# Turning the third of four squared MLP blocks with VectorE and ScalarE instead of TensorE, and taking the weight groups of the first down product in the order 0, 1, 3, 2

## The reference, cut to what matters

```python
u = _rmsnorm(h, norm_mlp_g)          # 256 x 2048
a = einsum('sd,df->sf', u, w_up)     # 256 x 8192
a = square(relu(a))
h = h + einsum('sf,fd->sd', a, w_down)
```

## Time and profile before

| | |
|---|---|
| median of 3 runs | 2249.17 us (2249.11 to 2249.85) |
| profiled execution, its own time | 2250.41 us |
| its span in the profile | 2248.7 us |
| granted TensorE clock, mean | 0.998 |
| instructions | 28778 |
| TensorE matmul busy | 2230.3 us |
| VectorE busy | 1642.7 us |
| ScalarE busy | 1149.5 us |

### The profile page before, as it was taken

The page is one execution under the profiler, slowest core; times in us unless marked ns, Lnnn a source line. Parts: engine busy times, 40 slices in busy tenths (PEclk is TensorE's granted clock), DMA queues, the critical chain, the costliest instruction groups (busy, mean ns, idle before and its releaser), DMA issues.

```text
span 2248.7 us, 28778 instructions
## 1 busy us (share of the span) xinstructions
PE 2230.3 (99%) x10115; PEld 1841.4 (82%) x10115; DVE 1642.7 (73%) x2156; ACT 1149.5 (51%) x1500; POOL 226.6 (10%) x369
## 2 busy tenths in 40 slices
PE   9999999999999999999999999999999999999998
PEld 7888888888888888888878877878888888888886
DVE  7998789988988988998788774656555545555556
ACT  5446457446546645645565744544443344434444
POOL 0111001111111111111011000001110011100110
PEclk9999999999999999999999999999999999999999
DMA  8983678988887898887678663656665666655663
GB/s 310 325 270 123 207 249 297 326 275 296 293 303 271 277 314 279 276 275 259 219 238 256 224 198 113 226 168 203 209 198 191 220 197 203 206 189 189 207 192 124
DMA packets 250109, 527.97 MB, mean 235 GB/s; under 512 B 22258, under 2 KB 22658, under 8 KB 248704
## 3 DMA queue, kind: packets, MB, share of 16 engines
q1 hardware_dynamic: 214256, 405.32, 54.7%
q0 software_dynamic: 33776, 116.17, 15.0%
q10 hardware_dynamic: 1952, 4.85, 0.6%
HBM read 517.87 MB, written 4.21 MB: 232 GB/s over the span
## 4 chain that ended last, share of the span: by engine, by line
PE 96%; DVE 2%; ACT 1%; issue 0%; DMA 0%; ACTq 0%; DVEq 0%; POOLq 0%
PE acc L1981 30%; PE acc L1985 30%; PE acc L1990 30%; PE tp L2053 1%; DVE wlo L1176 1%; PE acc L2004 0%; PE acc L2009 0%; PE acc L2014 0%; PE tp L2367 0%; PE tp L2385 0%; PE tp L2379 0%; PE acc L2037 0%; PE acc L2036 0%; PE acc L2035 0%; PE m L2174 0%
## 5 line engine op out<-in xcount | busy, mean ns | idle before, releaser
L609 ACT ACTIVATE whi<-wring 128x1024 fp32r<-128x1024 f32 x756 | 796.4, 1060 | 930.9 <-PE acc L1990 929.7
L1176 DVE TENSOR_TENSOR wlo<-wring,whi 128x1024 fp32r<-128x1024 f32 x754 | 909.6, 1225 | 439.5 <-ACT whi L609 438.2
L1981 PE MATMUL acc<-whi,xhi 128*128 128x512 f32 x2056 | 556.1, 392 | 0.1
L1985 PE MATMUL acc<-whi,xlo 128*128 128x512 f32 x2056 | 549.8, 389 | 0.0
L1990 PE MATMUL acc<-wlo,xhi 128*128 128x512 f32 x2056 | 549.7, 389 | 0.0
L1985 PEld LDWEIGHTS acc<-whi,xlo 128*128 128x128 f32 x2056 | 386.0, 188 | 80.7
L1990 PEld LDWEIGHTS acc<-wlo,xhi 128*128 128x128 f32 x2056 | 386.0, 188 | 80.4
L1981 PEld LDWEIGHTS acc<-whi,xhi 128*128 128x128 f32 x2056 | 383.2, 188 | 82.4 <-issue 4.7
L1218 DVE SCALAR_TENSOR_TENSOR macc<-mring,csil,macc 128x512 f32<-128x512 f32 x480 | 344.3, 749 | 36.0 <-DMA mring<-w_mod 30.1
L493 POOL DMA_DIRECT2D mring<-w_mod x192 | 139.2, 725 | 1101.2 <-DVE macc L1218 1054.2
L1981 PE MATMUL acc<-whi,ahi 128*128 128x512 f32 x608 | 163.5, 391 | 0.0
(11 more groups left out here) (296 smaller groups left out, 1335.2 us busy)
## 6 DMA issues: line engine op xcount, KB each, us to landing
wring<-w_up SPq DMA_DIRECT2D x216, 512.0 KB, 5.0
wring<-w_down SPq DMA_DIRECT2D x216, 512.0 KB, 5.7
mring<-w_mod POOLq DMA_DIRECT2D x192, 512.0 KB, 5.5
wring<-w_in SPq DMA_DIRECT2D x184, 512.0 KB, 5.0
wring<-w_gate SPq DMA_DIRECT2D x88, 512.0 KB, 4.4
wring<-w_out SPq DMA_DIRECT2D x64, 512.0 KB, 5.0
tmpT<-blk POOLq DMA_DIRECT2D x128, 32.0 KB, 3.2
gbig<-ctx_in POOLq DMA_DIRECT2D x2, 1024.0 KB, 6.5
```

The costliest lines, as they stand in the source:

```text
L609: act.activation(whi[:, piece_slot(c, piece), 0:half], wring[:, g4, piece * half:(piece + 1) * half], ACT.Copy).then_inc(hi_done, 1)
L1176: dve.tensor_tensor(wlo[:, h4, 0:half], wring[:, g4, piece * half:(piece + 1) * half], whi[:, h4, 0:half].bitcast(F32), ALU.subtract).then ...
L1981: pe.matmul(acc[:, 2 * pair + t, :], hi[:, tile, t * P:(t + 1) * P], whi[:, h4, w], start=(tile == starts), stop=False)
L1985: pe.matmul(acc[:, 2 * pair + t, :], lo[:, tile, t * P:(t + 1) * P], whi[:, h4, w], start=False, stop=False)
```

## The change

Block 2 is turned like blocks 0 and 1, by VectorE and ScalarE; only block 3 is left to TensorE. TensorE issues the 8 transposes of block 3 after group 16 instead of after group 17. The weights of the first down product (and of it alone) are loaded and multiplied in the order 0, 1, 3, 2, so that group 18 contracts over block 3 and group 19 over block 2. Ahead of the first group TensorE waits for the remainders of blocks 0 and 1, as before; ahead of group 18 it now waits for both `tp` banks, ahead of group 19 for the remainders of block 2. On ScalarE both late moves of block 2 stand between steps 16 and 17, and its rounding stands behind `round_banks` of block 3 after step 17. On VectorE, at step 17, `remain_banks` of block 3 stands first and `remain_relu` of block 2 behind it. The other edits are counts of the banks and of the blocks.

```diff
-MLP_MOVED = 2
+MLP_MOVED = 3
+MLP_ORDER = (0, 1, 3, 2)
...
-                    block_of(w_down, n * NB, kg0=i * 4)
+                    block_of(w_down, n * NB, kg0=i * 4, order=MLP_ORDER if n == 0 else None)
...
                     if 2 <= j <= MLP_MOVED + 1:
                         move_relu(2)
+                    if j == MLP_MOVED + 1:
+                        move_relu(3)
                     round_group(4 * j + 1)
                     if first and j == 0:
                         root(1)
+                    if 2 <= j <= MLP_MOVED:
+                        move_relu(3)
+                    if j == MLP_MOVED + 1:
+                        round_banks(xhi, 4 * MLP_MOVED, 2)
                     if 2 <= j <= MLP_MOVED + 1:
-                        move_relu(3)
                         round_relu(4 * (j - 2))
-                    if MLP_MOVED < j <= 4:
-                        round_banks(xhi, 4 * (j - 1), 2)
...
                     if g % 4 == 1 and 1 <= j <= 4:
+                        if j > MLP_MOVED:
+                            remain_banks(xhi, xlo, 4 * MLP_MOVED, 2)
                         if 2 <= j <= MLP_MOVED + 1:
                             remain_relu(4 * (j - 2))
                         if j <= MLP_MOVED:
                             turn_relu()
                         c.add("blk")
-                        if j > MLP_MOVED:
-                            remain_banks(xhi, xlo, 4 * (j - 1), 2)
...
                     for kg in range(3):
                         if j == 4 and kg == 0:
-                            pe.wait_ge(relu_lo, c.at("rs", KG * MLP_MOVED, KG))
-                        multiply(hi, lo, (kg,), 4, pair)
+                            pe.wait_ge(relu_lo, c.at("rs", KG * (MLP_MOVED - 1), KG))
+                        elif j == 4 and kg == 2:
+                            pe.wait_ge(tp_free, c.at("q", 2))
+                        order = MLP_ORDER if j == 4 else tuple(range(4))
+                        multiply(hi, lo, (order[kg],), 4, pair, order=order)
...
-                        if kg == 1 and MLP_MOVED < j <= 4:
-                            pe.wait_ge(blk_ready, c.at("blk", j))
+                        if kg == 0 and j == 4:
+                            pe.wait_ge(blk_ready, c.at("blk", 4))
                             turn_rows(blk, 2)
                         turn_ctx(4 * j + kg)
-                    if j == 4 or (first and j == 0):
+                    if first and j == 0:
                         pe.wait_ge(tp_free, c.at("q", 2))
-                    multiply(hi, lo, (3,), 4, pair)
+                    elif j == 4:
+                        pe.wait_ge(relu_lo, c.at("rs", KG * MLP_MOVED, KG))
+                    multiply(hi, lo, (order[3],), 4, pair, order=order)
```

## The result

The changed kernel takes 2275.03 us (median of 4 runs, 2274.89 to 2275.19), the kernel before in the same comparison 2249.51 us (2249.11 to 2251.09). The ratio is 1.0109, with a 95% interval of 1.0096 to 1.0121: 25.5 us slower. The forecast was 2267.8 us with a range of 2262 to 2272. The sign, the place and the length of the stop came as forecast; the time lies above the range.

The account below looks back on a forecast made before the run. The prediction took TensorE's matmuls to bound the kernel, busy 2230.3 of 2248.7 us. Stops of 18.9 less transposes of 3.6, plus 3.3 for the clock, gave +18.6 on 2249.17: 2267.8 us, range 2262 to 2272.

Parts of the forecast that it names:

- The transposes, 3.6 us won: On TensorE, block 2's 8 transposes go, 0.91 us in each of 4 chunks: 3.6 us less.
- The stop, 18.9 us: TensorE waits after group 17 for VectorE's backlogged `remain_banks`, 4.61 to 4.75 us a chunk: 18.9 us over four.
- that bare chain: Lower bound of the stop with VectorE free, 3.7 us; as the no-backlog rival 2260 us, chance 0.05.
- ScalarE ready by a hair: On ScalarE, block 3 is ready 5.38 us after its product, hidden by group 16's 5.44.
- No cost of `remain_relu`, no stop ahead of group 19: At VectorE's step 17, four `remain_relu`, 1.43 us together, lie beside group 18 and cost nothing.
- The clock, 3.3 us: TensorE's clock may fall at the four stops, 1.63 us each; half of 6.5 us taken, 3.3.
- TensorE busy for less: Expected sign in the changed profile: TensorE's busy time falls while the span grows; no size given.
- The sum: Stops of 18.9 less transposes of 3.6 give +15.3 us; with 3.3 for the clock, +18.6.
- the likeliest case: Stop ahead of group 18 bound by VectorE, no to four clock falls: 2264.5 to 2271.0 us, chance 0.84.
- the rival of the clock taking more: Clock falls at each stop and stays low twice as long, 3.3 us each: +28 us, 2277, chance 0.07.
- matmuls slow for more than 4 us after a stop: Sign on TensorE that would prove the clock term wrong: slow matmuls lasting over 4 us behind a stop.

Follow-up runs that it names:

- order alone: Kernel before with only the order 0, 1, 3, 2 and block 3's transposes after group 16; TensorE still turns block 2: 2275.76 us, ratio 1.0111.
- ScalarE first: Changed kernel with only ScalarE's rounding of block 3's banks moved ahead of its step 17: 2275.3 us, ratio 1.0111.
- VectorE first: Changed kernel with only VectorE's remainders of block 3's banks moved ahead of its step 17: 2266.21 us, ratio 1.0067.
- The run with 20 filling matmuls: Changed kernel with 20 small matmuls into an unused bank ahead of TensorE's wait at group 18: 2268.57 us, ratio 1.0079.
- the last version: Changed kernel with block 3's banks and block 2's strips taken ahead of step 17 on both engines: 2248.66 us, ratio 0.9993; timed again 2248.38 us, 0.9987.
- move alone: Changed kernel with the old group order 0, 1, 2, 3, and block 2 done ahead of block 3 at step 17: 2275.92 us, ratio 1.0112.
- the banks taken early: Changed kernel with only block 3's banks rounded and their remainders taken ahead of step 17, on both engines: 2250.73 us, ratio 1.0002.

## Why the prediction was wrong, point by point

- *The transposes, 3.6 us won*: right as a term, but only together with the stop. VectorE sets the time at which group 18 starts, so what TensorE saves ahead of it makes the stop longer by as much: order alone issues block 2's transposes, has a stop of 3.9 instead of 4.7 us, and starts group 18 at 417.70 against 417.56. With the stop removed, 2.0 and 2.6 us were measured.
- *The stop, 18.9 us*: 18.7 measured, at the place, by the releaser and for the reason given. ScalarE first and VectorE first confirm the two chains: 4.7 us by VectorE's queue, and behind it 3.1 to 3.2 us of lost time (3.0 of idle time) by ScalarE's. The prediction had 3.7 for that bare chain, with a remainder of weights in it that VectorE does not have to make first once its order is changed.
- *ScalarE ready by a hair*: right. The transposes start at 406.44, 0.04 after the set at 405.49 would have ended, and nothing follows from it.
- *No cost of `remain_relu`, no stop ahead of group 19*: right; TensorE's only waits in the chunks are the four.
- *The clock, 3.3 us*: **this is the step that failed**. I priced a fall at 1.63 us, from the one fall in the trace of before, and took half of four. I also described that place by two waits, 1.49 and 1.20 us; there is a third, of 1.08 us for VectorE's `h`, ahead of them (at 1511.11). The clock fell at all four stops, for 2.24, 1.71, 1.48 and 2.87 us, 8.3 in sum, and the fall at the opening of the second block's MLP cost 1.4 us more than before. That is 9.7 us for a term of 3.3. The one fall I had was near the cheap end of a spread of 1.5 to 3.0 us, and taking half had no row behind it. The run with 20 filling matmuls shows that the slow sets are the lowered clock: the same stop at a clock of 1.00 brings the next sets at their pace. For the same reason the sign "TensorE busy for less" did not come: it is busy for 6.8 us more. The Trainium skill ("TensorE: Matmul & The Clock Gate", HAM oscillation — how this bites in real kernels), which has a loop with such a wait pay for the return of the clock in every pass, was the better guide here: the loop paid in every pass, 1.5 to 2.9 us each time. With idle times of 3.0 and 2.3 us it paid in two passes of four.
- *The sum*: 15.3 was 15.1 by the trace. With 9.7 for the clock it would have been 2249.17 + 15.3 + 9.7 = 2274.2, against 2275.03. The measured case lies between the likeliest case and the rival of the clock taking more, for which I had taken double the price of one fall and a chance of 0.07. That rival's sign, matmuls slow for more than 4 us after a stop, was met at the first stop (4.96 us) and the fourth (6.50), and not at the other two.

What stays open is why the opening of the second block's MLP pays 1.4 us more in this kernel. Its code and its waits (1.49 and 1.20 us) are unchanged. In the run with ScalarE first the same place has two slow sets, of 1.87 and 1.47 us, in order alone it pays 3.0 us again, and in both profiled executions of the last version no set there is slow. So the price varies at a place that no edit touches, from nothing to 3.0 us, and the 1.4 may be the luck of two executions; no run isolates it. Nor does any run take out the doubled multiply-adds of steps 8 to 15: that VectorE's queue sets the end of the stop is shown, that these are what makes the queue late is read from the code and the timeline alone.

## What to carry to other kernels

When a consumer is moved forward by one step, the producers' place in their own queues must move too: here the transposes went one group earlier, but the two engines that pass their result on still took it behind a step that waits for the group just ended, or that comes late by their own load. Read for each new wait the time at which its last producer is done today, and subtract the time at which the consumer now wants it. And where this makes an engine of dense matmuls stop, price the clock with the stop, at every pass of the loop. Take for the price the whole spread of the falls that the traces show, and not a fraction of one.

## What the runs showed of the hardware that I had not expected

All counts here are of the stops in one profiled execution of each run. An idle time of TensorE ahead of dense matmuls made the granted clock fall to 0.50 in 12 of 12 cases at 4.5 to 4.8 us (the changed kernel, ScalarE first, move alone), in 4 of 4 at 3.7 us, in 2 of 4 at 3.0 us and in none of 6 at 0.3 to 0.5 us (the four short stops with the banks taken early, two more with VectorE first). At 2.3 us, with 2.4 us of small matmuls just before it, it fell in 2 of 4. The same kernel met both outcomes at one length. The extra time of a fall was 1.5 to 3.0 us, and did not shrink with the idle time: 8.3 us for four falls at 4.5 us, 8.1 at 3.7 us.

Small float32 matmuls of an identity by itself, 128 columns, took 0.22 us each and kept the clock up; the transposes of the same width took about 0.11.
